# Decode stage of a decoder step: gate weights in two buffers and ahead in the queues, value products laid between gate products

## What is computed

```
u = RMSNorm(h);  z = u @ W_in        # q/k/v of 12 dilated heads, q/k/v of 8 stick-breaking heads, 2 gate blocks
h += W_out( sigmoid(g_a) * W_oa(DilatedSWA(u)) + sigmoid(g_b) * W_ob(StickBreaking(u)) )
h += HierMoE(RMSNorm(h))
h += sigmoid(RMSNorm(h) @ W_pg) * (p @ W_pp)

def dilated_sample(q, k, v, buf, win, dil, slopes):   # one new token, rows of a window cache
    s = einsum(q, kg) * hd**-0.5 - slopes * dil * j
    p = softmax(s);  o = einsum(p, vg)
def stick_breaking(q, k, v, ...):                     # 256 cached rows in 2 pages, and the new token
    z = einsum(q, k) * hd**-0.5 + bias
    log_1mb = where(causal, -softplus(z), 0);  suffix = cumsum from the right
    a = where(causal, exp(-softplus(-z) + suffix - log_1mb), 0);  o = einsum(a, v)
```

## Time and profile before

| | us |
|---|---|
| median of 3 runs | 2178.96 (2177.6 to 2183.96) |
| the profiled execution's own time | 2174.56 |
| span in its profile | 2172.8 |
| TensorE busy, share of the span | 84% |
| mean granted TensorE clock | 0.906 of full speed |
| first gate weights issued in this stage | 443.2 |
| first gate product of the stage | 453.98 |
| last gate product begins | 591.28 |
| first matmul of the next stage | 603.01 |

### The profile page before, as it was taken

One profiled execution on the slowest core, in us unless ns is written; L12 is line 12 of the kernel. 1 busy time (PEld: TensorE's weight loads), 2 busy tenths in 40 slices (PEclk: granted clock), 3 DMA queues, 4 the chain that ended last, 5 costly groups with the idle time before them and its releaser, 6 DMA issues. The chain is left out here.

```text
span 2172.8 us, 27019 instructions
## 1 busy us (share of the span) xinstructions
PE 1834.6 (84%) x9708; PEld 1480.1 (68%) x9708; DVE 1111.3 (51%) x1513; ACT 878.6 (40%) x1256; POOL 129.1 (6%) x186
## 2 busy tenths in 40 slices
PE   5999999957888888766598991699999999994798
PEld 4999999957766666544494541577777777772585
DVE  5211111123159999632341223677777777771674
ACT  4111111111056776233430000566666666661454
POOL 0111111120000000000030003000000000001110
PEclk7999999977789999876699995799999999996799
DMA  3344333294045120410244114999999999984521
GB/s 117 107 124 125 120 116 116 95 260 157 27 139 162 49 69 11 169 27 11 72 153 148 58 41 175 370 409 396 391 397 398 397 392 398 393 348 172 185 77 40
DMA packets 158667, 402.80 MB, mean 185 GB/s; under 512 B 18619, under 2 KB 96043, under 8 KB 138116
## 3 DMA queue, kind: packets, MB, share of 16 engines
q1 hardware_dynamic: 123906, 320.71, 39.9%
q10 hardware_dynamic: 24370, 47.34, 6.0%
q0 software_dynamic: 10320, 33.82, 5.4%
HBM read 326.86 MB, written 82.64 MB: 188 GB/s over the span
## 5 line engine op out<-in xcount | busy, mean ns | idle before, releaser
L88 PE MATMUL p_acc<-uh,p_wl 128*128 128x344 f32 x720 | 234.9, 326 | 13.0 <-DVE ul L294 8.9
L90 PE MATMUL p_acc<-uh,p_wh 128*128 128x344 f32 x720 | 230.7, 320 | 0.0
L89 PE MATMUL p_acc<-ul,p_wh 128*128 128x344 f32 x720 | 230.5, 320 | 0.0
L306 DVE COPY p_zk<-p_tp 128x512 f32<-128x512 f32 (+1 forms) x90 | 44.2, 547 | 304.4 <-PE p_tp L227 304.4
L2138 DVE TENSOR_TENSOR x_wgl<-x_wg,x_wgh 128x2048 fp32r<-128x2048 f32 x64 | 143.9, 2290 | 54.5 <-ACT x_wgh L2077 54.5
L270 ACT ACTIVATE p_zc<-p_acc 128x344 f32<-128x344 f32 x90 | 41.2, 458 | 321.7 <-PE p_acc L90 321.7
L2138 DVE TENSOR_TENSOR x_wul<-x_wu,x_wuh 128x2048 fp32r<-128x2048 f32 x64 | 143.8, 2289 | 17.8 <-ACT x_wuh L2077 17.8
L88 PEld LDWEIGHTS p_acc<-uh,p_wl 128*128 128x128 f32 x720 | 135.9, 189 | 18.0 <-issue 15.0
L2077 ACT ACTIVATE x_wgh<-x_wg 128x2048 fp32r<-128x2048 f32 x64 | 119.2, 1917 | 46.4 <-DMA x_wg<-in_w_gate 46.4
L90 PEld LDWEIGHTS p_acc<-uh,p_wh 128*128 128x128 f32 x720 | 136.0, 189 | 0.0
L89 PEld LDWEIGHTS p_acc<-ul,p_wh 128*128 128x128 f32 x720 | 135.9, 189 | 0.0
(11 more groups left out here) (337 smaller groups left out, 4043.2 us busy)
## 6 DMA issues: line engine op xcount, KB each, us to landing
x_wg<-in_w_gate SPq DMA_DIRECT2D x64, 1024.0 KB, 8.2
x_wu<-in_w_up SPq DMA_DIRECT2D x64, 1024.0 KB, 8.0
x_wd<-in_w_down SPq DMA_DIRECT2D x32, 2048.0 KB, 12.6
x_x<-xs SPq DMA_DIRECT2D x32, 512.0 KB, 11.8
ys<-x_y ACTq DMA_DIRECT2D x32, 512.0 KB, 10.7
zT<-p_zc ACTq DMA_DIRECT2D x30, 516.0 KB, 3.5
p_w<-in_w_in SPq DMA_DIRECT2D x30, 512.0 KB, 5.5
ztok<-p_zk POOLq DMA_DIRECT2D x30, 512.0 KB, 4.6
```

What stands on the lines that cost most here:

```text
L88: pe.matmul(out, w_low, m_high, start=first, stop=False)
L89: pe.matmul(out, w_high, m_low, start=False, stop=False)
L90: return pe.matmul(out, w_high, m_high, start=False, stop=last)
L306: dve.tensor_copy(zk[0:r, b, t0:t0 + m, :], tp[j % 2][0:r, 0:m, :]).then_inc(zk_full, 1)
```

## The change

Four edits, all in `decode_and_gates`:

1. `g_w` gets a second buffer, in a part of the scratch tensor that is free in this stage. ScalarE issues the first two chunks' loads at the stage's start and the load of chunk c + 2 once chunk c is cut.
2. SP waits for the first gate weights before its first copy.
3. The value products are no longer issued in runs. `gates` takes a function that it calls after each of a group's eight slices; it issues one token's value products there. The dilated ones lie in group 8, all stick-breaking ones in group 16.
4. On VectorE the dilated scores go from step 2 to step 3 (behind the cut of chunk 2), the stick-breaking scores to steps 8 to 11, two batches each, the dilated heads' sums (`own_heads`) from step 8 to 9, and the stick-breaking ones from step 19 to 17.

```diff
-        S_SCORES = {9: (0, 1), 10: (1, 3), 11: (3, 5), 12: (5, 8)}
+        S_SCORES = {8: (0, 2), 9: (2, 4), 10: (4, 6), 11: (6, 8)}
...
-        gw = sb("g_w", [P, KD, P])
+        gw = [sb("g_w", [P, KD, P])[:, :, :],
+              flat2[:, (CB + 1) * NT:(CB + 1) * NT + KD * P].rearrange("p (k n) -> p k n", k=KD)]
...
+            sp.wait_ge(gw_in[0], 16)
             cached(sp, K, 0, 0, kq_in)
...
-                if n == D_SCORES_T - 4:
+                if n == D_SCORES_T - 3:
                     dilated_scores(0)
                     dilated_scores(1)
...
             def cut(c):
-                act.wait_ge(gw_in, 16 * (c + 1))
+                act.wait_ge(gw_in[c % 2], 16 * (c // 2 + 1))
                 need(act, acc_full, (c - 1) * NSPLIT)
-                act.activation(gwh[:, c % 2, :, :], gw[:, :, :], ACT.Copy).then_inc(gwh_full, 1)
-                if c + 1 < chunks:
+                act.activation(gwh[:, c % 2, :, :], gw[c % 2], ACT.Copy).then_inc(gwh_full, 1)
+                if c + 2 < chunks:
                     act.wait_ge(gwl_full, c + 1)
-                    load_gate(c + 1)
+                    load_gate(c + 2)
...
             load_gate(0)
+            load_gate(1)
             act.dma_start(table[:, :], g["page_table"].rearrange("(a b) p -> a (b p)", a=1)).then_inc(table_in, 16)
...
-                last.then_inc(acc_full, 1)
...
+                    if kk == KD - 1:
+                        last.then_inc(acc_full, 1)
+                    if between:
+                        between(kk)
...
+            def outputs_T(b, o, rows_, weights, heads, full):
+
+                for c in range(o.shape[1]):
+                    for x in range(2):
+                        last = pe.matmul(o[:, c, b, :], rows_(x, b)[:, c * P:(c + 1) * P],
+                                         weights[:, x, b * heads:(b + 1) * heads], start=(x == 0), stop=(x == 1),
+                                         skip_group_check=True)
+                if b == DEC - 1:
+                    last.then_inc(full, 1)
...
                 if n < GROUPS:
-                    gates(n)
+                    laid = {D_VALUES: lambda b: outputs_T(b, oT_ps, lambda x, t: V[:, x, t, :], pT, H_G, oT_full),
+                            S_VALUES: lambda b: outputs_T(b, eoT_ps, lambda x, t: PV[:, t, x, :], aT, H_B, eoT_full)}
+                    gates(n, laid.get(n))
```

More of the change, by code:

```diff
@@ L1134, in decode_and_gates @@
         ek_in = [sem(f"e_k_in{b}") for b in range(DEC)]
-        gw_in = sem("g_w_in")
+        gw_in = [sem(f"g_w_in{j}") for j in range(2)]
         g_out = [sem(f"g_g_out{j}") for j in range(2)]
@@ L1255, in cut @@
                 dve.wait_ge(gwh_full, c + 1)
-                dve.tensor_tensor(gwl[:, c % 2, :, :], gw[:, :, :], gwh[:, c % 2, :, :],
+                dve.tensor_tensor(gwl[:, c % 2, :, :], gw[c % 2], gwh[:, c % 2, :, :],
                                   ALU.subtract).then_inc(gwl_full, 1)
@@ L1327, in _ @@
                     dve.tensor_copy(pT[:, :, :], pT_ps).then_inc(pT_read, 1)
-                if n == D_VALUES:
+                if n == D_VALUES + 1:
                     own_heads(oaT[:, :, SEQ:NT], oT_ps, oT_full, H_G)
@@ L1336, in _ @@
                     dve.tensor_copy(aT[:, :, :], aT_ps).then_inc(aT_read, 1)
-                if n == STEPS - 1:
+                if n == S_VALUES + 1:
                     own_heads(obT[:, :, SEQ:NT], eoT_ps, eoT_full, H_B)
@@ L1342, in load_gate @@
             def load_gate(c):
-                act.dma_start(gw[:, :, :], win_v[:, :, QKV + c * P:QKV + (c + 1) * P]).then_inc(gw_in, 16)
+                act.dma_start(gw[c % 2], win_v[:, :, QKV + c * P:QKV + (c + 1) * P]).then_inc(gw_in[c % 2], 16)
             def cut(c):
-                act.wait_ge(gw_in, 16 * (c + 1))
+                act.wait_ge(gw_in[c % 2], 16 * (c // 2 + 1))
                 need(act, acc_full, (c - 1) * NSPLIT)
-                act.activation(gwh[:, c % 2, :, :], gw[:, :, :], ACT.Copy).then_inc(gwh_full, 1)
-                if c + 1 < chunks:
+                act.activation(gwh[:, c % 2, :, :], gw[c % 2], ACT.Copy).then_inc(gwh_full, 1)
+                if c + 2 < chunks:
                     act.wait_ge(gwl_full, c + 1)
-                    load_gate(c + 1)
+                    load_gate(c + 2)
             def evict(grp):
@@ L1394, in _, with gates @@
         def _(pe):
-            def gates(grp):
+            def gates(grp, between):
                 c, x = divmod(grp, NSPLIT)
@@ L1439, in _ @@
                     last.then_inc(aT_full, 1)
[L1440 to L1447, removed]
+                if n == S_VALUES:
+                    pe.wait_ge(aT_read, 1)
+                    pe.wait_ge(ev_in, 16 * DEC * PG)
                 if n < GROUPS:
-                    gates(n)
+                    laid = {D_VALUES: lambda b: outputs_T(b, oT_ps, lambda x, t: V[:, x, t, :], pT, H_G, oT_full),
+                            S_VALUES: lambda b: outputs_T(b, eoT_ps, lambda x, t: PV[:, t, x, :], aT, H_B, eoT_full)}
+                    gates(n, laid.get(n))
 def merge(nc, g):
```

1 line of the change is left out of this document (removed).

## The result

| kernel | median us (range) | ratio to before, 95% interval | span in its profile |
|---|---|---|---|
| before, 6 runs | 2180.41 (2175.91 to 2183.96) | | 2172.8 |
| changed, 6 runs | 2155.53 (2152.53 to 2163.32) | 0.9894 (0.9873 to 0.9915) | 2161.6 |

The change saves 1.06%, about 23 us (24.9 us between the two medians); the forecast was 10.9 us. The profiled execution of the changed kernel took 2163.32 us and is the slowest of its six, so its span says less than its stage.

A forecast was written before the change was run, and what follows sets the result against it. The bound was the decode stage's longest chain: TensorE stops for late gate weights and VectorE's scores, with K and Q right behind. Stage end 580.7 against 591.6 gave 10.9 us less, 2178.96 - 10.9 = 2168 us; range 2158 to 2175.

The forecast's parts named there:

- a new stop in place of two: TensorE, ready at 475.2, waits for the dilated scores until 486.0: 10.8 us in place of stops of 5.39 and 2.92.
- blocks: Three gate products plus one token's value products; in group 16 2.30 us at full clock and 4.35 at half.
- Rival (1): Group 8 keeps its clock, group 16 doesn't: stage ends at 575.0, kernel 2162 us; chance 0.15.
- (2): Groups 8 and 16 both keep full clock: stage ends at 560.9, 30.7 us less, kernel 2148 us; chance 0.08.
- Rival (3): Clock already down when the laid stretches begin: 4.3 us more each, kernel 2177 us; chance 0.09.
- Rival (4): First gate weights land as late as before, all 4.3 us later: kernel 2172 us; chance 0.06.
- (5): K and Q land at 495.6 at a 40% lower rate, stage ends 8.3 us after today: 2187 us; chance 0.05.
- packet for packet that is the same company: K and Q share the queues with chunks 2 and 3's weights instead of the first weights, so land 4 us later, 476.4.
- The third weights, put at about 468: Chunk 2's gate weights, started with the broadcast at about 449, come at about 468 and cost nothing unless later than K.
- it lies 4.4 us (0.2%) under the median of the runs, so I forecast 2178.96 - 10.9: The profiled execution, 2174.56 us, lies below the median; the stage's 10.9 us gain is taken off the median: 2168 us.
- the range's low end: Whole kernel at 2158 us: group 8 keeps its clock, group 16 doesn't, and K lands 4 us early.

The follow-up runs named there:

- second thin one: The first thin kernel with its stick-breaking value products over two groups (16 and 17, four per slice) instead of three: 2151.59 us, ratio 0.9875.
- first thin kernel: The changed kernel with value products laid more thinly, dilated over groups 8 and 9, stick-breaking over groups 15 to 17: 2135.97 us, ratio 0.9806.
- late broadcast: The changed kernel with the 2 MB broadcast of stick-breaking queries issued behind chunk 2's cut, not at the stage's start: 2151.79 us, ratio 0.9879.

## Why the prediction was right in its steps and wrong in its size

**What held.** The first gate product at 449.17 (forecast 449.5); no stop after chunk 0; a new stop in place of two, 9.23 us (10.8), released by K and Q and not by a cut; no stop for the softmax; scores 9.6 us behind K and Q; a fall of the clock in the middle of groups 8 and 16 with TensorE busy; blocks of 2.26 and 4.27 us (2.30 and 4.35). Rival (1), group 8 at full clock, is out, since the clock fell at 496.56, and (2) too. Rival (3) is out, since the clock was at full when both laid stretches began. Rival (4), the first weights as late as before, is out by the first gate product, and (5) by K and Q.

The Trainium skill ("TensorE: Matmul & The Clock Gate", the part on the HAM clock gate) says that activity releases the throttle and idling brings it back. The windows 544.35:571.66 of the changed kernel and 540.60:564.60 of the second thin one disagree: TensorE was busy for all of both (27.31 and 24.00 us), with a granted clock of 0.50. The first thin kernel shows that it isn't the value products as such either.

**The first step that failed: "packet for packet that is the same company".** K and Q were put at 476.4 and landed at 473.00, 3.4 us early. Packet for packet was right wherever both queues moved; what was wrong is that the other queue's transfers would stay where they were. The broadcast took 17.6 us from issue to landing before. In the changed kernel, of tile e_wide:

```profile
L1368 ACTq DMA_DIRECT2D e_wide<-ztok x1: 392/392/392, 444.7 to 444.7; - x1
...
DMA to landing us min/median/max: 10.7/10.7/10.7
```

And the DMA queues of the changed kernel (packets, MB, share of 16 engines), for 442.9:450, where only ScalarE's moved, then for 451:451.5 and for 452:456:

```profile
q10 hardware_dynamic: 2551, 2.01, 86.1%
...
q10 hardware_dynamic: 60, 0.12, 71.2%
q1 hardware_dynamic: 59, 0.06, 34.8%
...
q10 hardware_dynamic: 663, 0.77, 55.2%
q1 hardware_dynamic: 670, 0.69, 50.8%
```

ScalarE's queue had the engines to itself not only while SP waited: SP issued its first copy at 446.80, but none of its packets moved before 450. By then 2.01 MB of ScalarE's queue were through, the first two chunks' weights and about half of the broadcast; from 451 on the two share one to one. So K and Q began to move some 6 us later than before (in 444:444.5) and still landed only 0.5 us after the 472.53 at which VectorE had taken them. The broadcast was through at 455.4 instead of 462.1, and in 456:464 SP's queue moved 1.78 MB beside 0.60, where before in 456:462 it was 0.73 beside 0.97. The third weights, put at about 468, landed early by the same step, 11.0 us after their issue at 449.15. I had moved SP's transfers back by 3.9 us and left the other queue's end where it was. That the company decides is shown by the late broadcast, which brought K and Q 5.5 us forward. It is not the amount alone, though: from 450 to 473 ScalarE's queue moved 2.90 MB beside SP's 4.10, before, from 444 to 472, 3.15 beside 4.48, and the engines moved 305 GB/s for 273. Why they were quicker is open. All this is also why the wait costs less than it looks.

**The other terms of the stage**, nearly all a little short: groups 6 and 7, from the scores' transposes at 482.64 to group 8, 9.9 us (10.5); group 8 with its values 16.8 (17.1), its clock falling earlier than assumed but its half-speed blocks shorter; the stick-breaking scores end at 526.43, 17.1 us after group 8's last laid product (18.5), because ScalarE's eviction and cut need only the last gate product, which begins 1.9 us before the last laid ones are through; groups 13 to 15 with both transposes take 12.0 (12.3); group 16 takes 28.8 (30.5), since the clock stayed up for 5.9 us of it and not 4.8; group 17 6.0 (5.8). With the 3.4 us of K and Q, the last gate product ends at 573.3 where the forecast had 580.7, 7.4 us early. From there to the next stage it is 0.8 us longer than before, and the gain at the start of the next stage is 17.5 us instead of 10.9.

**The second step that failed: the base.** "it lies 4.4 us (0.2%) under the median of the runs, so I forecast 2178.96 - 10.9" takes a gain worked out on one execution and hangs it on the median, as if the 4.4 us lay in stages that don't change. The two further executions of before show that 5.5 to 8.1 us of the spread lie in the decode stage itself, the one that the change rebuilds. By their mean the gain up to the next stage is 22 us, so the 5 us or so between 17.5 and 23 are most likely of that kind; three profiles don't show it for certain. And the range's low end (2158, measured 2155.53), built from K and Q 4 us early and a clock that stays up in group 8, never had this term in it, though the row for it (profiled time and median) stood in the table.

**A judgement that the runs correct.** The working took the clock's fall as given once value products are there, and never priced their spread as a choice. It is the largest term of the stage: 20 us, nearly as much as the whole change (23). As the change lays them, the products cost time: in runs the stage was 2.0 us shorter.

## What to carry to other kernels

When a wait is put ahead of one queue, work out the other queue anew as well: it runs alone for that time and gives the engines back sooner, so the delayed transfers can lose less than the wait (here 0.5 us for 3.6). Before a gain in one stage is hung on a median, ask in which stage the profiled execution differs from it, and profile the base more than once if the stage has clock changes in it. And where many tiny matmuls must run, spread them thinly between large ones and read the granted clock for the whole stretch: the spread was worth more here (20 us) than the earlier scores (10.0), the second buffer (5.4) or the wait (4.8).

## What the runs showed of the hardware that I had not expected

- Issuing eight bias copies of a few bytes held ScalarE for 4.59 us in the changed kernel and for 11.01 us without SP's wait; the engine's next cut waited for that issue, not for its weights, which had landed 4.8 and 13.1 us after their own issue at 443.4.
- SP's queue moved no packet for 3.2 us after its first issue (446.80) while ScalarE's queue was at work on earlier copies, and shared one to one from 451 (60 packets to 59 in 451:451.5).
- TensorE's clock fell in stretches without a gap (at 496.56 and 544.35 in the changed kernel, at 540.60 in the second thin one) and stayed full for 68.27 us in the first thin kernel, which does the same products in the same stage.
- The same program's decode stage took 149.0, 157.4 and 154.6 us, while the changed one's took 136.3 and 136.2. Why the former varies and the latter does not is open; it was seen in few executions.
